# Last group of two expert stages worked token tile by token tile, and half a pair of late down matrices loaded ahead into spent parameter space

## What is computed

```
# layers 0 and 1: 4 groups x 4 experts, hidden 256 (top 1 group, top 2 experts in it)
x = layer_norm(ALPHA * x + mix, ln_mix_g, ln_mix_b)
h = silu(x @ w_gate[e]) * (x @ w_up[e])
ffn = sum over e of  c[token, e] * (h @ w_down[e])
x = layer_norm(ALPHA * x + ffn, ln_ffn_g, ln_ffn_b)
# layer 2: 4 groups x 8 experts, hidden 512, RMS norms
h = h + moe(rmsnorm(h));  out = rmsnorm(h, final_norm_w)
```

## Time and profile before

| | |
|---|---|
| median of 3 runs | 1193.12 us (1191.11 to 1197.55) |
| the profiled execution, its own time | 1190.23 us |
| span of its trace | 1188.2 us |
| mean granted TensorE clock | 0.982 |
| TensorE matmuls busy | 1087.6 us (92%) |
| VectorE, ScalarE busy | 333.3 us, 221.9 us |
| moved by DMA | 364.02 MB, mean 306 GB/s |
| expert stage 0, from the first gate product to the last scatter | 173 to 292 us |
| expert stage 1 | 450 to 569 us |
| expert stage 2 | 740 to 1179 us |

### The profile page before, as it was taken

One profiled execution on the slowest core, in us unless ns is written; L12 is line 12 of the kernel. 1 busy time (PEld: TensorE's weight loads), 2 busy tenths in 40 slices (PEclk: granted clock), 3 DMA queues, 4 the chain that ended last, 5 costly groups with the idle time before them and its releaser, 6 DMA issues.

```text
span 1188.2 us, 14623 instructions
## 1 busy us (share of the span) xinstructions
PE 1087.6 (92%) x5890; PEld 547.0 (46%) x5890; DVE 333.3 (28%) x991; ACT 221.9 (19%) x499; POOL 1.0 (0%) x6
## 2 busy tenths in 40 slices
PE   9998999999999999999999989987976798788895
PEld 5555455554787546554464545422421242224231
DVE  1576463113013445111523655100100010001002
ACT  2145331111024422111122232100100010001011
POOL 0000000000000000000000000000000000000000
PEclk9999999999999999999999999999998998899999
DMA  9886138999733136999653148999999999999995
GB/s 319 178 224 245 72 143 367 411 421 393 274 117 140 71 129 241 414 422 402 221 211 142 71 169 318 378 403 428 430 425 430 426 429 427 430 429 427 428 427 223
DMA packets 81886, 364.02 MB, mean 306 GB/s; under 512 B 22530, under 2 KB 27940, under 8 KB 57892
## 3 DMA queue, kind: packets, MB, share of 16 engines
q1 hardware_dynamic: 81028, 363.04, 77.4%
q10 hardware_dynamic: 800, 0.17, 0.1%
HBM read 362.14 MB, written 1.05 MB: 306 GB/s over the span
## 4 chain that ended last, share of the span: by engine, by line
PE 68%; DMA 23%; DVE 5%; ACT 2%; issue 1%; SPq 1%; ACTq 0%; DVEq 0%
DMA weights<-in_expert_w_down_dram 17%; PE bank L1305 16%; PE bank L873 9%; PE bank L895 7%; PE bank L1346 5%; PE bank L1357 4%; PE bank L860 4%; DMA weights<-in_expert_w_up_dram 4%; PE bank L1394 3%; PE bank L885 2%; DMA weights<-in_expert_w_gate_dram 2%; PE bank L848 2%; PE bank L837 2%; PE bank L1247 1%; PE bank L1027 1%
## 5 line engine op out<-in xcount | busy, mean ns | idle before, releaser
L1305 PE MATMUL bank<-weights,projected 128*64 128x256 f32 (+1 forms) x2048 | 348.9, 496 | 37.3 <-DMA weights<-in_expert_w_gate_dram 21.2
L1305 PEld LDWEIGHTS bank<-weights,projected 128*64 128x64 f32 (+1 forms) x2048 | 137.7, 125 | 233.5 <-issue 187.2
L873 PE MATMUL bank<-weights,x_transposed 128*128 128x512 f32 x256 | 118.8, 607 | 0.9 <-ACT heads_transposed L1796 0.9
L895 PE MATMUL bank<-weights,mixed 128*128 128x512 f32 x192 | 89.7, 604 | 1.6 <-DVE mixed L2378 1.0
L1357 PE MATMUL bank<-weights,work 128*32 128x512 f32 x448 | 57.1, 643 | 26.5 <-DMA weights<-in_expert_w_down_dram 22.0
L2564 DVE TENSOR_TENSOR work<-work,bank 64x512 f32<-64x512 f32 (+1 forms) x24 | 16.4, 682 | 203.6 <-PE bank L1305 203.6
L873 PEld LDWEIGHTS bank<-weights,x_transposed 128*128 128x128 f32 x256 | 46.7, 192 | 51.3 <-issue 49.4
L1902 ACT ACTIVATE work<-bank 128x512 f32<-128x512 f32 (+1 forms) x32 | 19.0, 594 | 245.8 <-PE bank L1357 187.9
L1394 PE MATMUL bank<-work,heads_transposed 128*128 128x512 f32 x120 | 56.2, 605 | 4.2 <-ACT work L1902 4.2
L1346 PE MATMUL bank<-weights,work 128*32 128x512 f32 x512 | 57.0, 594 | 1.5 <-ACT projected L1851 1.5
L2544 DVE COPY work<-bank 64x512 f32<-64x512 f32 (+1 forms) x30 | 20.7, 690 | 119.4 <-PE bank L1357 77.9
(11 more groups left out here) (350 smaller groups left out, 1056.7 us busy)
## 6 DMA issues: line engine op xcount, KB each, us to landing
weights<-in_expert_w_gate_dram SPq DMA_DIRECT2D x30, 2048.0 KB, 17.3
weights<-in_expert_w_up_dram SPq DMA_DIRECT2D x30, 2048.0 KB, 18.7
weights<-in_expert_w_down_dram SPq DMA_DIRECT2D x24, 2048.0 KB, 20.6
weights<-in_moe_w_gate_dram SPq DMA_DIRECT2D x16, 2048.0 KB, 11.1
weights<-in_moe_w_up_dram SPq DMA_DIRECT2D x16, 2048.0 KB, 12.1
weights<-in_moe_w_down_dram SPq DMA_DIRECT2D x16, 2048.0 KB, 10.2
weights<-in_sb_w_in_dram SPq DMA_DIRECT2D x6, 2048.0 KB, 17.6
weights<-in_w_in_dram SPq DMA_DIRECT2D x6, 2048.0 KB, 13.5
```

Of the source, the lines that this page charges most:

```text
L873: i = mm(BANK[6 + t][:, :], XT[:, kt, t * P:(t + 1) * P], w[:, kt, :], start=kt == 0, stop=kt == KT - 1)
L895: i = mm(BANK[bank][:, :], mixT[:, kt, t * P:(t + 1) * P], w[:, kt, :], start=kt == 0, stop=kt == KT - 1)
L1305: i = mm(b[n_slots * c:n_slots * (c + 1), e * F:(e + 1) * F], x[:, kt, q * n_slots:(q + 1) * n_slots], w[c][:, col:col + F], start=kt == 0 ...
```

## The change

Six things are changed.

1. In stages 0 and 1 the last group has an order of its own (`last_group_by_tile` in the PE, ACT and DVE blocks): gate and up of tile 0, then half of gate of tile 1, the transposes of tile 0's hidden rows, the rest of gate of tile 1, both downs, residual and scatter of tile 0, and then up, downs and scatter of tile 1. DVE and ACT run tile 0's whole norm within the group. The outputs go to `LAST_DOWN_BANK` (the old table). Every gate and up product now has 32 stationary columns, so four stand side by side, with 256 moving columns.
2. `DOWN_BANK` for the other groups sends tile 0 to banks 1 and 0, tile 1 to 2 and 3; the wait for the gathered rows moves from a = 0 to a = 1.
3. The filler matmuls behind stages 0 and 1 are taken out.
4. In stage 2 half of the pair of down matrices of unit 2 (`SLICE_UNIT`) of the last group, the columns for f = 0 and 1 of both chunks (2 x 1 MB), is loaded ahead into `small_params`, `misc` and `norm_params` (`load_slices`), and the chunk loads of that pair bring the other half only.
5. The norm weights of stages 0 and 1 are issued before the flag is read; `load_norm(6)` now waits until TensorE is through the down products of unit 2 of the last group.
6. Some semaphores of the first attention are merged, and names in `small_params` and `misc` are laid out anew. The path that is not taken gets a second norm of tile 0 (`again`).

```diff
+        DOWN_BANK = {(0, 0): BANK[1], (0, 1): BANK[0], (1, 0): BANK[2], (1, 1): BANK[3]}
+        LAST_DOWN_BANK = {(0, 0): BANK[2], (0, 1): BANK[3], (1, 0): BANK[1], (1, 1): BANK[0]}
...
+        SLICE_UNIT = 2
+        SLICE_PARTS = [[SMALL[:, 2000 - 3 * CH:2000], NORM_[:, 0:CH]], [MISC[:, 2200 - 3 * CH:2200], NORM_[:, CH:2 * CH]]]
...
                     load_extra(1, (0,))
+                    load_slices(0, 1)
+                    load_slices(1, 1)
+                    load_slices(1, 0)
                     sp.wait_ge(logits_psum, T * NMOE)
+                    load_slices(0, 0)
                     load_extra(3, (0,))
...
-                            load_unit_chunk(G - 1, j, True)
+                            load_unit_chunk(G - 1, j, True, 2 * D if j // 2 == first_chunk(units, "down", SLICE_UNIT) // 2 else 0)
...
             moe(2)
+            sp.wait_ge(chunk_done, chunk_no(2, (G - 1) * 6 * UNITS[2] + first_chunk(UNITS[2], "down", SLICE_UNIT) + 2, True))
             load_norm(6, (a["final_norm_w_2"],))
...
-                        if a == 0 and u == units - 1 and not last:
+                        if a == SPLIT[L] and u == units - 1 and not last:
...
+                    def hidden_of_tile(kind, a, k0, k1, w):
+
+                        bank, o = BANK[0 if kind == "gate" else 1], a * F
+                        for kt in range(k0, k1):
+                            if kind == "gate" and a == 0:
+                                rows_copied(kt)
+                            for q in range(4):
+                                e, c = q // 2, q % 2
+                                col = e * KT * F + kt * F
+                                i = mm(bank[cap * q:cap * (q + 1), o:o + F], x[:, kt, q * n_slots + cap * a:q * n_slots + cap * (a + 1)],
+                                       w[c][:, col:col + F], start=kt == 0, stop=kt == KT - 1)
+                                if kt == KT - 1 and a and q >= 2:
+                                    i.then_inc(chunk_done, 1)
+                        if k1 == KT and a == 0:
+                            i.then_inc(tile0_psum, 1)
...
+                    def last_group_by_tile():
+
+                        gate = load("gate", 0)
+                        hidden_of_tile("gate", 0, 0, KT, gate)
+                        up = load("up", 0)
+                        hidden_of_tile("up", 0, 0, KT, up)
+                        pe.wait_ge(p_ready, g * 2 + (2 * G * L + 2))
+                        for t in range(T):
+                            i = nc.tensor.transpose(BANK[2][:, t * P:(t + 1) * P], PW[:, t * WP:t * WP + P], ident)
+                        i.then_inc(pwT_psum, 1)
+                        pe.wait_ge(tile0_silu, L + 1)
+                        hidden_of_tile("gate", 1, 0, 4, gate)
+                        hidden_T_of_tile(0)
+                        hidden_of_tile("gate", 1, 4, KT, gate)
+                        pe.wait_ge(pwT_act, g + (G * L + 1))
+                        down_of_tile(0, 0)
+                        down_of_tile(0, 1)
+                        add_residual(L, 0, 0)
+                        add_residual(L, 0, 1)
+                        scatter(0, 0, 0)
+                        scatter(0, 0, 1)
+                        hidden_of_tile("up", 1, 0, KT, up)
+                        add_residual(L, 1, 0)
+                        hidden_T_of_tile(1)
+                        add_residual(L, 1, 1)
+                        down_of_tile(1, 0)
+                        down_of_tile(1, 1)
+                        scatter(0, 1, 0)
+                        scatter(0, 1, 1)
...
-            keep_clock_up(1, 1)
             project_first(N_SB, 6, 2, by_k(X), KT - 2)
...
-            keep_clock_up(6, 1)
             project_first(N_2, 12, 4, by_k(U), KT)
...
+                def last_group_by_tile(g):
+
+                    act.wait_ge(tile0_psum, 3 * L + 1)
+                    ac(SG[:, 0:CH // 2], BANK[0][:, 0:CH // 2], ACT.Silu).then_inc(tile0_silu, 1)
+                    act.wait_ge(pwT_psum, g * pwT_banks + (pwT0 + 1))
+                    ac(PWT[:, 0, :], BANK[2][:, 0:S], ACT.Copy).then_inc(pwT_act, 1)
+                    act.wait_ge(chunk_done, g * per_group + (chunk_no(L, first_chunk(units, "gate", 0), True) + 2))
+                    ac(SG[:, CH // 2:CH], BANK[0][:, CH // 2:CH], ACT.Silu).then_inc(silu_done, 1)
+                    nc.scalar.preload_act_table_set("natural_log_exp_and_others")
+                    outputs(g, 0, LAST_DOWN_BANK)
+                    rstd_from(1 if L == 0 else 3, (0,))
+                    outputs(g, 1, LAST_DOWN_BANK)
+                    if L == 1:
+                        rstd_from(4, (0,))
+                    last_outputs(g, 1, LAST_DOWN_BANK[1, 1])
...
+                def last_group_by_tile(g):
+
+                    dve.wait_ge(tile0_silu, L + 1)
+                    dve.wait_ge(tile0_psum, 3 * L + 2)
+                    tt(HB[:, 0:F], SG[:, 0:F], BANK[1][:, 0:F], ALU.mult).then_inc(tile0_hidden, 1)
+                    dve.wait_ge(tile0_psum, 3 * L + 3)
+                    cp(HT[:, 0:F], BANK[3][:, 0:F]).then_inc(tile0_hidden, 1)
+                    outputs(g, 0, True, LAST_DOWN_BANK)
+                    dve.wait_ge(acc_half, L + 1)
+                    statistics(0, (0,), from_psum=True)
+                    dve.wait_ge(acc_ready, 2 * L + 1)
+                    statistics(0, (1,), from_psum=True)
+                    ask_rstd("layer", 0)
...
+                    norms(0, second_tile, second_transposed)
```

More of the change, by code:

```diff
@@ L137 @@
 OUT_DMAS = 3
+AGAIN_VAR = (3, 13)
+AGAIN_DONE = (9, 18)
 def loaded_value(n):
@@ L1351, in down @@
                                     pe.wait_ge(last_quarter[f], 16 * 2)
+                                sliced = extra and u == SLICE_UNIT and f < 2
+                                if extra and u == SLICE_UNIT and f == 2:
+                                    load("down", u)
                                 for hh in range(2):
@@ L1401, in scatter @@
                             i.then_inc(acc_ready, 1)
+                    if last and SPLIT[L]:
+                        last_group_by_tile()
+                        return
                     for u in range(units):
@@ L2532, in gathered_others, with outputs @@
                         i.then_inc(xc_dve, 1)
-                def outputs(g, pair, last=False):
+                def outputs(g, pair, last=False, banks=DOWN_BANK):
                     if L == 2 and last and pair < 2:
@@ L2551, in group @@
                 def group(g, last):
+                    if last and split:
+                        last_group_by_tile(g)
+                        return
                     dve.wait_ge(pwT_psum, g * pwT_banks + (pwT0 + pwT_banks))
@@ L2572, in group @@
                             outputs(g, u - 1, last)
-                    if last and L < 2:
-                        transposed(g, units - 1)
-                    elif not last:
+                    if not last:
                         gathered(g + 1, lambda: transposed(g, units - 1))
-                    for pair in range(units - 1 if units > 1 else 0, pairs - 1 if last and split else pairs):
+                    for pair in range(units - 1 if units > 1 else 0, pairs):
                         outputs(g, pair, last)
```

245 lines of the change are left out of this document (155 added, 90 removed).

## The result

| | before | changed |
|---|---|---|
| median, first comparison | 1192.58 us (1190.44 to 1197.55, 12 runs) | 1186.51 us (1184.14 to 1189.87, 12 runs) |
| median, second comparison | 1192.47 us (1189.16 to 1197.20, 25 runs) | 1188.04 us (1184.70 to 1189.76, 11 runs) |
| ratio, first | | 0.9947, interval 0.9937 to 0.9958 |
| ratio, second | | 0.9954, interval 0.9937 to 0.997 |
| profiled execution, span | 1190.23, 1188.2 us | 1188.33, 1186.5 us; second time 1187.75, 1186.0 us |

The ratios are to the kernel before, with a 95% interval. The changed kernel is about 0.5% faster: 6.1 us by the first comparison, 4.4 by the second. The two profiled executions differ by only 1.9 and 2.5 us from that of before.

The account below looks back on a forecast made before the run. TensorE was taken to bound the kernel until about 776 us, then DMA transfers. A front of 5.5 less 0.5 for slices, plus 2.1 at the end, gave 7.1 us: forecast 1186.0, range 1181.5 to 1191.0.

Parts of the forecast that it names:

- Stage 1's last group: Stage 1's end: tile 1's products begin at s + 41.9 instead of s + 45.65, s being the group's start; gain 3.7 us.
- the narrow products: Last groups' gate and up: 0.056 us a record, four side by side; rival that they do not: 1213 us, chance 0.04.
- Stage 0: Stage 0's last group: one filler of 0.9 us goes, the order loses 0.4; gain 0.5, ends 0 and 0.9.
- it can only be lost where DMA becomes late: Other groups of stages 0 and 1: condition for losing the 1.3 us from free banks; ends 0.5 and 1.3.
- the later release of gate and up slots is paid by nobody: Last groups: slots free at s + 11.4 and 22.2, not 7.1 and 14.5; next needed chunks are at s + 31 or later.
- The other groups: Three gathering groups per stage: down products' waits for ACT vanish with free banks, 0.22 x 6 = 1.3 us.
- Front: Up to about 776 us, where TensorE sets the pace: stage 1, stage 0 and other groups together bring 5.5 us.
- Slices, in front: Stage 2's front: 4.9 us of slice transfers mostly fit idle DMA room; 0.5 us left over, ends 0.2 and 2.3.
- End: Last group's tail: with 4.9 us of bytes less ahead, PE can use 2.1 us before TensorE is the bound.
- Final norm's weight: Kernel's end: `load_norm(6)` issued about 1167.8 costs nothing; rival that it lands up to 4 us late, 1188 to 1190, chance 0.06.
- the clock in stage 1's gap: Rival: without fillers TensorE's clock falls in stage 1's gap, price 1.7 to 3.5 us, time about 1188.5; chance 0.08.
- Little room: Rival: slices find little room by busy share, flag and roots cost DVE 1 us more; gain 4.3, time 1188.8; chance 0.22.

Follow-up runs that it names:

- the swap alone: The kernel before with the new banks of the down products in the groups that gather, nothing else: 1189.35 us, ratio 0.9968.
- the same edit: Changed kernel with half of tile 1's up products ahead of tile 0's downs in stage 0's last group, DVE's order untouched: 1187.03 us, ratio 0.9953.

## Why the prediction was right or wrong

The time, the range and the sign were right; of the sum one step was wrong and two were mis-sized, so the nearness of the time is in part luck. All is counted in the traces, with dips of the clock left aside.

- **Stage 1's last group**: forecast 3.7, measured 3.02. Without the 0.65 of DMA wait it is 3.67, so the walk through DVE's queue, the narrow products, the flag (0.90 for 1.0) and the added wait (0.18 for 0.3) were right.
- **Stage 0**: forecast +0.5, measured -1.5. This is the step that failed, "it can only be lost where DMA becomes late", together with "the later release of gate and up slots is paid by nobody". I asked which slot is released later, and not which matrix is wanted sooner. Tile 0's downs begin at s + 13.1 here (s + 11.6 without the wait) instead of s + 17.0, with the DMA engines at a share of 1.0 ahead of it. The wait is 1.4 of the 2.0 that are missing. Without it the stretch takes 31.9, no less than before, so the order itself costs PE 0.9 there, not 0.4, and eats the filler's 0.9 whole. The ends of 0 and 0.9 did not hold it; they needed one for a down chunk that has not landed.
- **The other groups**: forecast 1.3 with 1.3 as the upper end, measured 1.9. The idle column says 0.22, but the products before the downs also run their ends out before the stall and it has to start anew. The second group of stage 0, before and with the swap alone:

```profile
220.05 1.96 PE L1247 MATMUL bank<-heads_transposed,projected 128*128 128x128 f32 x16
222.22 7.07 PE L1346 MATMUL bank<-weights,work 128*32 128x512 f32 x64 [0.22 <-ACT projected L1851]
```

```profile
218.63 1.96 PE L1248 MATMUL bank<-heads_transposed,projected 128*128 128x128 f32 x16
220.52 7.07 PE L1347 MATMUL bank<-weights,work 128*32 128x512 f32 x64
```

  Start to start it is 2.17 before and 1.89 with the swap: 0.28 for a stall of 0.22. In the first group of a stage the stall is 0.31 and costs 0.38 (2.27 and 1.89). So a stage loses 0.38 + 2 x 0.28 = 0.94, and two of them 1.9.
- **Front**: 3.7 + 0.5 + 1.3 = 5.5 forecast, 3.0 - 1.5 + 1.9 = 3.4 measured. At SP's load into `projected` it is 3.65 (704.39 to 700.74), since the changed kernel is 0.22 early already at stage 0's first gate product (172.79 for 173.01).
- **Slices, in front**: 0.5 left over forecast. From the load into `projected` to that of the second group it takes 71.85 us in the profile of before and 71.85 in the second one of the changed kernel, so TensorE paid nothing there. From there to the gate of unit 3 of the last group it takes 371.61 and 372.42: 0.8 left over, inside the ends 0.2 and 2.3. The windows moved 409 GB/s at 730 to 750 instead of 343, nearly the 408 that the shortfall by rate had.
- **End**: forecast 2.1, measured 2.13. That half of the slices, 2.5 us of transfers, gives no less follows from this step, and the forecast did not draw it.
- **Final norm's weight**: issued at 1168.28, costs nothing, as forecast.

So the sum was 3.4 - 0.8 + 2.1 = 4.7 and not 7.1. The median came out at 1186.5 all the same. The forecast's base was 1193.12, the median of three runs; twelve gave 1192.58. Less 4.7 that is 1187.9, near the second median, 1188.04, and 1.4 above the first. The sum was 2.4 too large, the base 0.5 too high, and the first median came out low: that the time met the forecast within 0.5 us is luck.

Of the rivals, the narrow products fall (0.056 a record), the clock in stage 1's gap falls, and so does the norm weight. "Little room" had the right sign: the gain was smaller, but the missing part sits in the two last groups and their waits for DMA, stage 0's above all, and not in DVE's flag.

## What to carry to other kernels

When an order is changed so that results come sooner, list what the moved work reads as well as what it frees: here a matrix was wanted 5 us sooner from transfers that had no slack. Fill such a gap with work that needs nothing late, and then follow the second engine's queue, since the same edit gave nothing in time until DVE's order was changed too. And bytes loaded ahead are worth only what the end can use: half of them did as much.

## What the runs showed of the hardware

- TensorE's clock dips now and then to 1.2 GHz in stretches where it had none in other executions of the same or nearly the same program. Up to 780 us the granted clock over 5 us was 0.66 at 70 to 75 in six of twelve profiles, 0.66 to 0.83 between 445 and 455 in four, 0.66 at 95 and 170 in one, 0.69 at 275 in one (behind the wait of 3.02), and 0.50 at 735 in one; none of these is in all. One at 70 goes with a stage 0 that is about 0.9 us late (261.35 to 261.71 against 260.47 to 260.52 in kernels with the same groups), the one at 450 cost 1.6, the one at 733 to 744 4.5. What sets it off no run here shows. It is enough to make one profiled execution 2 us slower than another, so a step of a sum is best compared from mark to mark within a stretch, and not by the span.
- How long stage 0's last group waits for its down matrices differs between executions: 1.44 and 1.73 in two of the same kernel, 3.02 in one with the same program up to there. The downs then begin at 274.44, 275.00 and 275.14: the longest wait is in the execution whose group began earliest (260.47 against 261.35). Counted from the stage's first gate product, the downs begin 101.65 to 103.22 us behind it in the five profiles with the new banks that wait, and 101.37 behind it with the old ones. So the banks, which bring TensorE to the last group 0.96 us sooner, do not bring the landing any sooner: in the changed kernel time won in the groups ahead comes back as a longer wait. What moves the landing by the 1.6 us between these profiles no run here shows.
